# The two transposes of an attention pair side by side, and a lower pace of the attention steps

## The reference, cut to what matters

```
# first attention (8 heads, 128 + 64 wide): s = (qn.kn + qr.kr) * scale; mask by 64-token chunks
# second (16 heads of 64, shared keys and values): s = q.k / 8 + bias[head]; the same kind of mask
# third: 8 heads of 64 with bias and causal mask, and 8 heads of stick-breaking attention
p = softmax(s);  o = p @ v;  y = o @ w_o
# stick-breaking: log_keep = log_sigmoid(-z) of past keys; a = exp(log_beta + later sums of log_keep)
```

## Time and profile before

| | before |
| --- | --- |
| median of 3 runs | 961.05 us |
| the profiled execution | 960.99 us |
| its span | 959.1 us |
| TensorE matmul busy | 944.2 us (98%) |
| VectorE busy | 718.9 us (75%) |
| ScalarE busy | 543.6 us (57%) |
| chain that ended last | PE 93%, ACT 3%, DVE 2%, DMA 1% |
| granted TensorE clock | 9 tenths or more in all 40 slices |

### The profile page before, as it was taken

How to read it: one execution, slowest core, us unless ns; L and a number is a source line. 1 busy time by engine, 2 the same in 40 slices (tenths; PEclk the granted TensorE clock), 3 DMA queues, 4 the chain that set the end, 5 groups by cost and what they waited for, 6 DMA issues and landing times.

```text
span 959.1 us, 18737 instructions
## 1 busy us (share of the span) xinstructions
PE 944.2 (98%) x7890; PEld 911.9 (95%) x7890; DVE 718.9 (75%) x1332; ACT 543.6 (57%) x845; POOL 17.8 (2%) x51
## 2 busy tenths in 40 slices
PE   9999999999999999999999999999999999999997
PEld 9989999999998988899999998998999999999996
DVE  7875897787569777799888789655656789888653
ACT  7755654444447366565444554556756576766542
POOL 0000000000000000000000000000320000000000
PEclk9999999999999999999999999999999999999999
DMA  9645487667736734268768892653344636555621
GB/s 341 231 169 206 166 281 249 233 251 270 256 134 220 263 132 139 83 224 314 295 227 290 317 329 75 258 176 133 107 143 147 220 132 220 183 213 179 217 89 44
DMA packets 28259, 195.62 MB, mean 204 GB/s; under 512 B 3216, under 2 KB 3600, under 8 KB 5264
## 3 DMA queue, kind: packets, MB, share of 16 engines
q1 hardware_dynamic: 28176, 194.43, 57.3%
HBM read 192.98 MB, written 1.05 MB: 202 GB/s over the span
## 4 chain that ended last, share of the span: by engine, by line
PE 93%; ACT 3%; DVE 2%; DMA 1%; issue 1%; SPq 0%; POOL 0%; DVEq 0%; ACTq 0%
PE bank L548 26%; PE bank L549 25%; PE bank L554 25%; PE bank L750 2%; PE bank L776 2%; PE bank L592 2%; PE bank L603 2%; PE bank L597 1%; PE bank L760 1%; PE bank L631 1%; PE bank L637 1%; PE bank L632 1%; PE bank L669 1%; PE bank L675 1%; PE bank L670 1%; DMA s_front<-in_front 1%
## 5 line engine op out<-in xcount | busy, mean ns | idle before, releaser
L1507 DVE TENSOR_TENSOR s_wlo<-s_raw,s_whi 128x512 fp32r<-128x512 f32 (+1 forms) x354 | 364.4, 1070 | 121.9 <-ACT s_whi L1017 121.7
L1017 ACT ACTIVATE s_whi<-s_raw 128x1024 fp32r<-128x1024 f32 (+2 forms) x226 | 299.5, 1353 | 193.6 <-PE bank L554 187.3
L548 PE MATMUL bank<-s_hh,s_whi 128*128 128x256 f32 x1392 | 390.2, 280 | 1.3 <-DVE s_wlo L1507 1.0
L549 PE MATMUL bank<-s_hl,s_whi 128*128 128x256 f32 x1392 | 384.8, 276 | 0.0
L554 PE MATMUL bank<-s_hh,s_wlo 128*128 128x256 f32 x1383 | 382.2, 276 | 0.0
L548 PEld LDWEIGHTS bank<-s_hh,s_whi 128*128 128x128 f32 x1392 | 261.4, 188 | 6.6 <-issue 4.2
L549 PEld LDWEIGHTS bank<-s_hl,s_whi 128*128 128x128 f32 x1392 | 261.5, 188 | 0.1
L554 PEld LDWEIGHTS bank<-s_hh,s_wlo 128*128 128x128 f32 x1383 | 259.7, 188 | 0.0
L548 PE MATMUL bank<-s_ph,s_whi 128*128 128x256 f32 x528 | 145.9, 276 | 0.0
L549 PE MATMUL bank<-s_pl,s_whi 128*128 128x256 f32 x528 | 145.7, 276 | 0.0
L554 PE MATMUL bank<-s_ph,s_wlo 128*128 128x256 f32 x525 | 144.9, 276 | 0.0
(11 more groups left out here) (274 smaller groups left out, 1288.6 us busy)
## 6 DMA issues: line engine op xcount, KB each, us to landing
s_raw<-in_gu SPq DMA_DIRECT2D x44, 1024.0 KB, 5.0
s_raw<-in_dn SPq DMA_DIRECT2D x33, 1024.0 KB, 4.9
s_raw<-in_wada SPq DMA_DIRECT2D x24, 1024.0 KB, 5.2
s_raw<-in_up SPq DMA_DIRECT2D x22, 1024.0 KB, 4.9
s_raw<-in_wo SPq DMA_DIRECT2D x8, 1024.0 KB, 4.9
s_raw<-in_win_g SPq DMA_DIRECT2D x8, 1024.0 KB, 4.9
s_raw<-in_mla SPq DMA_DIRECT2D x4, 1024.0 KB, 13.9
s_raw<-in_wkv_v SPq DMA_DIRECT2D x4, 1024.0 KB, 5.7
```

Of the source, the lines that this page charges most:

```text
L548: e.matmul(out, hi, xh[:, k, :], start=first, stop=False, skip_group_check=True)
L549: e.matmul(out, hi, xl[:, k, :], start=False, stop=False, skip_group_check=True)
L1017: e.activation(whi[w % SPLIT][:, at], src, ACT.Copy).then_inc(S.hi.tick((w, c0)), 1)
L1507: e.tensor_tensor(wlo[s][:, at], src, whi[s][:, at].bitcast(F32), ALU.subtract).then_inc(S.lo.tick((i, j), (i, "all")), 1)
```

## The change

In `_soft_steps`, turn (i+1, 1) now stands directly behind turn (i+1, 0), ahead of chunk i and exp i+2. The second turn of a pair needs no credit and costs none. The paces of wq1 and wo1 go from 0.35 to 0.27, that of win_q from 0.3 to 0.24. The paces of the first layer (`PACE0`) and of win_g stay, and so do banks, buffers and all instructions.

```diff
@@ _soft_steps
         for p in nxt:
             yield "turn", (p, 0)
+            yield "turn", (p, 1)
         for p in now:
             yield "chunk", p
         for p in new:
             yield "exp", p
-        for p in nxt:
-            yield "turn", (p, 1)
@@ _mixed
+    def free():
+        name, i = ahead[0]
+        return name in FREE or name == "turn" and i[1] == 1
+
@@ _mixed, the loop over units
-        while peek() is not None and (credit >= 1 or ahead[0][0] in FREE) and ready(n):
-            if ahead[0][0] not in FREE:
+        while peek() is not None and (credit >= 1 or free()) and ready(n):
+            if not free():
                 credit -= 1
             yield taken(n)
@@ _order1
-    return _mixed(_units("wq1") + _units("wo1"), _soft_steps(range(8)), {"wq1": 0.35, "wo1": 0.35},
+    return _mixed(_units("wq1") + _units("wo1"), _soft_steps(range(8)), {"wq1": 0.27, "wo1": 0.27},
@@ _order2
-                  {"win_q": 0.3, "win_g": 0.2}, lambda p: ("win_q", 16 * (p // 2) + 15), None)
+                  {"win_q": 0.24, "win_g": 0.2}, lambda p: ("win_q", 16 * (p // 2) + 15), None)
```

## The result

| | before | after |
| --- | --- | --- |
| median | 961.04 us (961.02 to 961.13) | 966.58 us (966.18 to 966.96) |
| ratio, with its 95% interval | | 1.0057 (1.0042 to 1.0072) |
| the profiled execution, its span | 960.99, 959.1 us | 966.33, 964.4 us |

The changed kernel is 0.6% slower. The direction was forecast; the size was not: 966.58 lies above the forecast of 963.9 and above the range's upper end of 965.2.

What follows compares the result with a forecast made beforehand. TensorE's stream was taken to bound the kernel, so only its work and waits count. The terms, -0.2 + 0.85 + 1.4 - 0.45 + 1.9 - 0.55 = +2.95 us, gave 963.9 us from 961.05; range 961.1 to 965.2.

Steps and rivals of the forecast that it cites:

- What bounds the kernel: Whole kernel: TensorE's own stream is the end, busy 944.2 of 959.1 us; edits count only by its instructions and waits.
- Term 1: All layers: a pair's transpose groups standing together save 0.015 us per pair, 14 undisturbed pairs, -0.2 us.
- Term 2: First layer: transposes (2, 0) wait for VectorE's read of scores 3, pair 3's second group for scaling; +0.85 us.
- Term 3: wo1 layer, pairs 0 and 1: both groups use bank 6, so the second waits for the first's eviction; +1.4 us.
- Term 4: wo1 layer, unit 40: its lag behind a split and low part falls from 1.4 to 0.95; -0.45 us.
- Term 5: wo1 layer, pair 7: GpSimd's bias2 mask stretches VectorE's scaling, so the second transposes wait; +1.9 us.
- Term 6: Third layer: values 2's wait goes (-0.35), joining scores 2 and values 0 saves 0.2, stick steps 0; -0.55 us.
- (a): wo1 layer, pair 7: mask and scaling miss each other, giving 962.1 us; chance 0.27.
- (b): All layers: changing between transposes and products is dear, sixteen pairs give -3.1 us; 959.2 with the mask missed; chance 0.05.
- (c): First and third layers: waits vanish, VectorE earlier, stick steps gain, mask missed; 961.05 us, no change; chance 0.1.
- (d): Third layer: sticks land badly against splits on top of the forecast, giving 964.5 us; chance 0.08.

Runs made afterwards that it cites:

- alone: The change in only the first or only the third attention layer, other layers as in the kernel before: 962.37 us and 962.45 us.
- the last two runs: Kernel before plus wo1 layer's new order, bank 0, bank 4, mask after values 7: 960.73 us; kernel before plus only bank 0 and that mask: 960.98 us.
- the version with all mends: Changed kernel, first layer's old order, wo1 second transposes (pairs 0, 1) in bank 0, values 6 bank 4, mask after values 7, win_g banks shifted: 961.11 us.

## Why the prediction was wrong, step by step

**What bounds the kernel: right.** TensorE's stream is the end, and every microsecond of new waiting in it reached the end (4.87 by layers, 5.09 in all).

**Term 1, groups together (-0.2): right.** Standing together saves a pair 0.015 to 0.02 us by the spacing of its instructions; after all waits were mended, about 0.2 was left for eight pairs. No run supports a dear switch.

**Term 2, first layer (+0.85, measured +1.17, alone +1.19 from scores 2 on): right in its mechanism.** Transposes (2, 0) start at 70.30 (forecast 70.1), released by the read of scores 3; those of pair 3 are held by the scaling's second half (1.01 instead of 0.82) and end at 77.1 (forecast 76.9). The 0.2 us that I took off for two joints of scores with values are not there: from scores 2 to the second product behind values 0 it is 3.87 us (from 55.12), and the two steps alone take 2.48 and 1.43, less a matmul of 0.115, which is 3.80. A further 0.1 is a longer wait for chunk 0's low part (0.48 at 62.24, before 0.38).

**Term 3, bank 6 (+1.4): right,** to a tenth: the transposes of pair 2 start at 355.39 instead of 352.73, 1.43 us more than the 1.23 by which the stretch starts later.

**Term 4, unit 40 (-0.45): this step failed, hidden in the total.** I followed the split and chunk 5's low part behind it to the unit that needs that chunk (40) and found the lag shorter, taking it that values 6 and unit 39 would be done while unit 40 waits. But values 6, now ahead of unit 40, write bank 7, which is free only when VectorE has read that same chunk out of it. So they wait with it, and their 0.80 us and the 0.345 of unit 39 come behind the wait: 1.15 us more. The lag at unit 41 is about 2.1 us net (387.26 against 383.91, less 1.23) instead of 0.95. So the term is +0.7, not -0.45.

**Term 5, mask and scaling (+1.9): the collision right, the price wrong, by the same step.** Less the 1.23, the mask starts at 384.99 (forecast 385.0) and the scaling ends at 387.43 (forecast 387.5). The Trainium skill ("SBUF — State Buffer", section "SBUF: two separate sides") has the shared ports as a lock for a whole instruction; the trace agrees again, with four scalings in 2.69 us beside a mask of 2.11. But I priced the wait from a TensorE that is on time. It was 1.15 us later than that, since values 6 had waited, and paid 0.78 more. Terms 4 and 5 came to 1.45 as forecast and to 1.43 as measured (2.86 less 1.43): that is luck, two errors with the same cause that cancel. The run with values 6 in another bank shows the true structure: there the price is 1.64.

**Term 6, third layer (-0.55, measured +1.23, or +1.30 alone): wrong, and this is the miss of the total.** The wait of values 2 did go, as forecast (-0.3). Three things stand against it. The unit of win_g behind win_q's last one waits 0.75 us, for I had looked only at what the moved step itself waits for, and not at what it had been hiding. The sticks' wait for GpSimd was 0.28 before, at values 6, and is 0.74 now, at values 5; I had written "-0.3 to +0.5, I take 0", with no reason for the 0. And transposes (1, 0) and (1, 1) take 1.01 us where 0.82 is the norm (0.19). With the 1.0 that the first wait costs in all, these are +1.65; less 0.35 for values 2 and 0.2 for the joint below, +1.1 of the 1.23. So the steps that failed are the -0.55 of this term, which has the new wait at win_g at nothing, and the stick steps taken at 0.

The Trainium skill ("TensorEngine Tiling (Array Packing)", section "Key Properties") says that a change of tiling mode drains TensorE. I took the 0.2 us per joint from the half-height steps of the wo1 layer. In the first layer, where values and half of the scores have the products' full shape, nothing was saved. In the third layer it was: from the last product before scores 2 to the second one behind values 0 it is 2.08 us (650.59 to 652.67), and before it was 1.29 and 1.23 for the two steps apart (646.53 to 647.82, 647.94 to 649.17), the same numbers as in the earlier trace rows.

**The rivals.** (a) did not happen: mask and scaling met in each trace of the new order with the new pace, except where the mask was held back. At the old pace they missed each other, at the price of other waits. (b) is excluded by the last two runs. (c) is excluded. (d), sticks landing badly, did happen, with 0.46 us in one stick step; it explains 964.5 and no more. The range was too narrow because it took the first and the third layer's waits as known from the waits in the table before. A reordering uncovers waits that are in no table.

**What stays open.** Of the first layer's loss about 0.3 us is not placed, and 0.1 of the third layer's; some matmul records are missing there. Why the stick step waits longer was not followed up. And the wait of values 5 in the third layer, the largest that is left in the version with all mends, was not tried by itself.

## What to carry to other kernels

When a step moves in a stream that is the bound, ask three things of it: what it waits for, what waits for it, and what it was hiding where it stood. The third is in no table of waits; read it by naming, for each pair of instructions that become neighbours, the bank or buffer that they hand over (here win_q's last unit and win_g's first; chunk 5's read and values 6, once unit 40 no longer stood between them).

Don't add up waits that share a chain. Two waits in front of one engine close together are in series: taking away either alone showed 0.8 and 0 us, both together 1.7. So an edit that wins nothing by itself isn't refuted before its neighbour is gone too.

A pairing that saves 0.02 us for each joint can't pay for one bank conflict of 1 us; give the second group its own bank first.

## What was not expected of the hardware

In the profiled execution of the kernel with values 6 in bank 4, TensorE was idle from 387.04 to 388.67, and its granted clock fell while it was: it is 1.00 up to 388.0, 0.92 over the next 0.3 us and 0.50 from 388.3 on. Windows of 4 us, columns as in the earlier trace rows:

```profile
384.00:388.00 4.00, 2.76 (x21) 1.91 (x20) 3.82 (x5) 2.13 (x10) 1.48 (x1) 1.00 0.76 248
388.00:392.00 4.00, 3.33 (x17) 3.33 (x18) 1.50 (x4) 1.26 (x3) 0.47 (x1) 0.57 0.44 186
```

and the transposes and products in it, PE:

```profile
388.67 1.54 PE L763 MATMUL bank<-s_ident,s_S 128*128 128x128 f32 x6 [1.64 <-DVE s_S L1584]
...
390.65 0.41 PE L551 MATMUL bank<-s_hh,s_whi 128*128 128x256 f32 x1
```

Six transposes take 1.54 us instead of 0.82, products start every 0.21 us instead of 0.115: the lower of the two levels, 1.2 GHz, until about 391.6. It cost 1.2 us (the layer at +4.05 instead of about +2.8), and the execution took 967.93 while the other three took 966.46 to 966.49. An idle of this size did not bring the clock down in the changed kernel (1.63 us before values 6) nor in the kernel with the old pace in the wo1 layer (up to 2.2 us). So in one execution of four here an idle stretch of 1.64 us cost its length almost twice. The kernel with the old pace had one execution of four at 968.45 us, the others at 966.59 to 967.10, with the same mean clock of 0.996 where the others have 0.998 or more; it may be the same, but it left no trace. What tips the clock in one execution and not in the next, no run here shows.
